# Five RMS norms: squares summed in four column groups of TensorE, three of them applied inside feed-forward units

## The reference

```python
def rmsnorm(x, g):
    xf = x.astype(jnp.float32)
    r = lax.rsqrt(jnp.mean(xf * xf, axis=-1, keepdims=True) + EPS)
    return (xf * r * g.astype(jnp.float32)).astype(x.dtype)

def modulate(h, shift, scale):
    return h * (1.0 + scale[:, None, :]) + shift[:, None, :]
```

## Time and profile before

| | |
|---|---|
| median of 3 runs | 1994.65 us (1994.48 to 1998.07) |
| profiled execution | 1996.98 us |
| its span | 1995.2 us |
| PE busy | 1930.8 us (97%) |
| POOL busy | 1303.9 us (65%) |
| DVE busy | 998.7 us (50%) |
| ACT busy | 805.7 us (40%) |
| mean granted TensorE clock | 0.991 of full speed |

### The profile page before, as it was taken

The page is one execution under the profiler, slowest core; times in us unless marked ns, Lnnn a source line. Parts: engine busy times, 40 slices in busy tenths (PEclk is TensorE's granted clock), DMA queues, the critical chain, the costliest instruction groups (busy, mean ns, idle before and its releaser), DMA issues.

```text
span 1995.2 us, 34548 instructions
## 1 busy us (share of the span) xinstructions
PE 1930.8 (97%) x13934; PEld 1767.5 (89%) x13934; DVE 998.7 (50%) x2150; ACT 805.7 (40%) x872; POOL 1303.9 (65%) x311
## 2 busy tenths in 40 slices
PE   6989899999999999999999898999999999999998
PEld 4879788877676899999999787899999999999998
DVE  6766455675754565445335546433344334654112
ACT  3443344344444543334334424433343334334332
POOL 5726257766667577777775421487758775868784
PEclk8999899999999999999999999999999999999999
DMA  8537167788997656665665311266656665655452
GB/s 348 215 145 274 50 280 305 279 324 324 364 361 271 269 193 252 248 229 219 237 247 201 155 64 64 106 254 239 244 190 252 234 252 190 254 211 211 174 185 85
DMA packets 63958, 448.76 MB, mean 225 GB/s; under 512 B 7680, under 2 KB 8800, under 8 KB 9824
## 3 DMA queue, kind: packets, MB, share of 16 engines
q1 hardware_dynamic: 61888, 441.65, 58.2%
q10 hardware_dynamic: 1952, 5.44, 0.7%
HBM read 446.01 MB, written 1.05 MB: 224 GB/s over the span
## 4 chain that ended last, share of the span: by engine, by line
PE 54%; issue 23%; POOL 18%; DMA 3%; DVE 1%; ACT 1%; POOLq 0%; SPq 0%; ACTq 0%; DVEq 0%
POOL W L670 15%; PE bank L747 11%; PE bank L749 11%; PE bank L748 11%; PE bank L1196 3%; PE bank L1264 3%; PE bank L1197 3%; PE bank L1204 3%; DMA raw<-in_pages 2%; POOL YC L723 1%; PE bank L773 1%; PE bank L782 1%; PE bank L1139 1%; PE bank L793 1%; PE bank L812 1%
## 5 line engine op out<-in xcount | busy, mean ns | idle before, releaser
L670 POOL TENSOR_TENSOR W<-raw,W 128x2048 fp32r<-128x2048 f32 x220 | 1013.7, 4613 | 497.1 <-ACT W L1564 497.0
L747 PE MATMUL bank<-YH,W 128*128 128x256 f32 x1936 | 551.2, 285 | 1.1 <-POOL W L670 0.8
L749 PE MATMUL bank<-YH,W 128*128 128x256 f32 x1936 | 547.6, 283 | 0.0
L748 PE MATMUL bank<-YL,W 128*128 128x256 f32 x1936 | 547.6, 283 | 0.0
L1564 ACT ACTIVATE W<-raw 128x2048 fp32r<-128x2048 f32 x220 | 420.2, 1910 | 302.3 <-PE bank L749 275.6
L747 PEld LDWEIGHTS bank<-YH,W 128*128 128x128 f32 x1936 | 371.0, 192 | 3.9 <-POOL W L670 1.2
L748 PEld LDWEIGHTS bank<-YL,W 128*128 128x128 f32 x1936 | 371.3, 192 | 0.4 <-issue 0.2
L749 PEld LDWEIGHTS bank<-YH,W 128*128 128x128 f32 x1936 | 371.2, 192 | 0.0
L1919 DVE SCALAR_TENSOR_TENSOR bank<-mraw,CA,bank 128x256 f32<-128x256 f32 x696 | 329.0, 488 | 19.8
L2016 DVE TENSOR_TENSOR bank<-bank,SIL 128x256 f32<-128x256 f32 x110 | 47.6, 433 | 541.0 <-ACT SIL L1583 541.0
L747 PE MATMUL bank<-HH,W 128*128 128x256 f32 x880 | 249.7, 284 | 0.5 <-DVE HL L2018 0.4
(11 more groups left out here) (383 smaller groups left out, 3053.2 us busy)
## 6 DMA issues: line engine op xcount, KB each, us to landing
raw<-in_pages SPq DMA_DIRECT2D x284, 1024.0 KB, 4.8
mraw<-in_mpages SPq DMA_DIRECT2D x98, 1024.0 KB, 6.9
R<-in_pages SPq DMA_DIRECT2D x20, 1024.0 KB, 6.9
XR<-in_pages SPq DMA_DIRECT2D x12, 1024.0 KB, 5.5
R<-in_mpages SPq DMA_DIRECT2D x4, 1024.0 KB, 16.5
HT<-in_acts ACTq DMA_DIRECT2D x1, 1024.0 KB, 14.3
CT<-in_mpages SPq DMA_DIRECT2D x1, 1024.0 KB, 19.6
raw<-in_mpages SPq DMA_DIRECT2D x1, 1024.0 KB, 25.4
```

The lines of the kernel that those rows point to most:

```text
L670: nc.gpsimd.tensor_tensor(WL[:, p % SLOTS, :], raw[:, p % SLOTS, :], WH[:, p % SLOTS, :].bitcast(f32), ALU.subtract).then_inc(s_lo, 1)
L747: mm(out, w[0], x[0], start=start, stop=False, skip_group_check=True)
L748: mm(out, w[0], x[1], start=False, stop=False, skip_group_check=True)
L749: return mm(out, w[1], x[0], start=False, stop=stop, skip_group_check=True)
```

## The change

For norms 2 to 6, PE no longer makes eight full 128x128 products with ones. `norm_groups` makes eight products with 32 columns of ones: tile k of the squares goes to the 32 output partitions 32*(k mod 4) and following, so that each group of 32 partitions holds the sum of two tiles. ACT copies the bank to `XR[:, 0, :]` (`norm_groups_copy`), and PE adds the four groups with one full product with ones (`norm_total`). Every value is then 32 times too large, and `norm_root` divides by that.

The parts are placed anew. Norm 2: groups in job 36, copy in job 36, total in job 37; its bank is 7 in place of 5, and PE waits for the last modulation sum of the stage in place of the third scatter. Norm 3: groups after unit 1 of `ctx_ff`, total inside unit 2 between its two gate and up pages. Norm 4: groups after unit 5, total in unit 6, low parts in unit 7. Norm 5: groups after unit 1 of `ff00`, total in unit 2, low parts in unit 3. In such a unit ACT takes the root between the two SiLUs and makes `norm_scaled` (for norm 3 also the squares of norm 4) between its second and third page split; DVE takes the gain between the two hidden halves, and the reciprocal and the eight tiles between the second hidden half and the modulation take and sum. The units that are touched are those whose modulation sum is for one vector. Norm 6: the groups are issued inside `kac0`, after 36 of its 48 matmuls, the total behind `kac0`; ACT takes the root ahead of the copy of `kac0`'s result. The pass `ff00` has two more units written out in place of looped.

```diff
-        tile("ss2", 1, (5,), "act")
+        tile("ss2", 1, (MISC,), "act")
...
+        GROUPED = (2, 3, 4, 5, 6)
+        TOTAL_IN = {("ctx_ff", 2): 3, ("ctx_ff", 6): 4, ("ff00", 2): 5}
+        LOWS_IN = {("ctx_ff", 7): 4, ("ff00", 3): 5}
+        MID_NORM = {"ctx_ff": ((2, "ss3"), (6, "ss4")), "ff00": ((2, "ss5"),), "ff01": (), "ff10": (), "ff11": ()}
...
+            def norm_groups(n):
+                ps = opened(pe, f"ss{n}")
+                pe.wait_ge(s_sq, NCH * (n + 1))
+                for k in range(KD):
+                    rows = slice(GW * (k % NG4), GW * (k % NG4 + 1))
+                    last = mm(ps[rows, 0:S], ONES[:, 0:GW], XR[:, k, :], start=(k < NG4), stop=(k >= KD - NG4),
+                              skip_group_check=True)
+                last.then_inc(s_grp, 1)
+
+            def norm_total(n):
+                pe.wait_ge(s_grpd, GROUPED.index(n) + 1)
+                mm(bank(f"ss{n}")[:, 0:S], ONES[:], XR[:, 0, :], start=True, stop=True, skip_group_check=True)\
+                    .then_inc(s_tile, 1)
...
+                        if behind is not None and b == 1 and k == k_tiles // 2:
+                            behind()
...
+                        if j == 0 and (name, u) in TOTAL_IN:
+                            norm_total(TOTAL_IN[name, u])
...
+                if t == NJOB - 4:
+                    pe.wait_ge(s_macc, MOD_AT["ctx_ff"])
+                    norm_groups(2)
                 if t == NJOB - 3:
-                    pe.wait_ge(s_scd, 4 * (GSLOTS - 2))
-                    norm(2)
+                    norm_total(2)
...
-            ff_pass("ctx_ff", 2, (lambda: mid_norm("ctx_ff", 1, 3), lambda: None, lambda: mid_norm("ctx_ff", 3, 4)))
+            ff_pass("ctx_ff", 2, (nothing, lambda: mid_norm("ctx_ff", 2, 3), nothing, nothing, lambda: mid_norm("ctx_ff", 6, 4)))
...
-            norm(6)
+                   behind=lambda: norm_groups(6)).then_inc(s_tile, 1)
+            norm_total(6)
...
+                copies = GW if n in GROUPED else 1
+                free(f(RT[:, 0:S], ps[:, 0:S], ACT.Sqrt, bias=EPSC[:, 0:1], scale=1.0 / (D * copies)), f"ss{n}")
+
+            def norm_groups_copy(n):
+                act.wait_ge(s_grp, GROUPED.index(n) + 1)
+                f(XR[:, 0, :], bank(f"ss{n}")[:, 0:S], ACT.Copy).then_inc(s_grpd, 1)
...
+                        if (name, u) in TOTAL_IN:
+                            mid = TOTAL_IN[name, u]
+                            if j == 0:
+                                norm_root(mid)
+                            else:
+                                norm_scaled(mid)
+                                if mid == 3:
+                                    norm_squares(4)
...
+                        if j == 0 and (name, u) in TOTAL_IN:
+                            norm_gain(TOTAL_IN[name, u])
+                    if (name, u) in TOTAL_IN:
+                        norm_coef(TOTAL_IN[name, u])
+                        norm_tiles(TOTAL_IN[name, u], range(KD), low=False)
+                    if (name, u) in LOWS_IN:
+                        for q in range(KD):
+                            norm_low(LOWS_IN[name, u], q)
```

More of the change, by code:

```diff
@@ L269, in first_view @@
             return buf.rearrange("p (k n) -> p k n", k=KD)
+        NG4, GW = 4, P // 4
         BY_DVE, BY_PE = (0, 2, 4, 6), (1, 3, 5, 7)
@@ L331, in build @@
         s_sq = sem("norm_squares")
+        s_grp, s_grpd = sem("norm_groups_summed"), sem("norm_groups_copied")
         s_rt, s_ri, s_xr, s_yf, s_y = (sem("norm_root"), sem("norm_coef"), sem("norm_scaled"), sem("norm_result"),
@@ L542, in build @@
                                                             (1, (BOTH, ONE)), (1, (BOTH, BOTH)), (1, (ONE, BOTH)))),
-                ("ff00", FF_UNITS, "y", "acc_00", ((1, (ONE, ONE)), (1, (ONE, ONE)), (FF_UNITS - 2, (ONE, ONE)))),
+                ("ff00", FF_UNITS, "y", "acc_00", ((1, (ONE, ONE)), (1, (ONE, ONE)), (1, (ONE, ONE)), (1, (ONE, ONE)),
+                                                          (FF_UNITS - 4, (ONE, ONE)))),
                 ("ff01", FF_UNITS, "y", "acc_01", ((2, (ONE, ONE)), (FF_UNITS - 2, (ONE, ONE)))),
@@ L814, in tile_page, with linear @@
                 return last
-            def linear(p, ps, x, ready=None, k_tiles=KD, wcol=FU, off=0, inc=True):
+            def linear(p, ps, x, ready=None, k_tiles=KD, wcol=FU, off=0, inc=True, behind=None):
                 w = shaped([a[:, 0:k_tiles * wcol] for a in arrived(p)], "p (k n) -> p k n", k=k_tiles)
@@ L1313, in mid_norm, with nothing @@
                 pe.wait_ge(s_modev, MOD_AT[name] + u - 1)
-                norm(n)
-            ff_pass("ctx_ff", 2, (lambda: mid_norm("ctx_ff", 1, 3), lambda: None, lambda: mid_norm("ctx_ff", 3, 4)))
+                norm_groups(n)
+            def nothing():
+                pass
+            ff_pass("ctx_ff", 2, (nothing, lambda: mid_norm("ctx_ff", 2, 3), nothing, nothing, lambda: mid_norm("ctx_ff", 6, 4)))
             ff_pass("ff00", 4, (lambda: None, lambda: mid_norm("ff00", 2, 5)))
             mod_product(MOD_AT["mixer"] - 1)
-            linear(PA["proj_a"], opened(pe, "kac0"), YC, inc=False, ready=lambda k: y_ready(5, k)).then_inc(s_tile, 1)
-            norm(6)
+            linear(PA["proj_a"], opened(pe, "kac0"), YC, inc=False, ready=lambda k: y_ready(5, k),
+                   behind=lambda: norm_groups(6)).then_inc(s_tile, 1)
+            norm_total(6)
             linear(PA["proj_a"] + 1, opened(pe, "kac1"), YC, inc=False).then_inc(s_tile, 1)
@@ L1545, in norm_root @@
                 ps = filled(act, f"ss{n}")
-                free(f(RT[:, 0:S], ps[:, 0:S], ACT.Sqrt, bias=EPSC[:, 0:1], scale=1.0 / D), f"ss{n}")
+                copies = GW if n in GROUPED else 1
[3 more added lines that the diff above has]
+                f(XR[:, 0, :], bank(f"ss{n}")[:, 0:S], ACT.Copy).then_inc(s_grpd, 1)
             def norm_scaled(n, ks=range(KD)):
@@ L1676, in _, with nothing @@
             after(PA["wout"] + 3)
-            def state_norm():
-                norm_result(3)
-                norm_squares(4)
+            def nothing():
+                pass
             def expert_split(u, part):
@@ L1765, in _ @@
                     norm_squares(2)
+                if t == NJOB - 4:
+                    norm_groups_copy(2)
                 if t == NJOB - 3:
@@ L1777, in _ @@
             norm_squares(3, "acc_moe")
-            ff_pass("ctx_ff", (state_norm, lambda: None, lambda: norm_result(4)))
+            ff_pass("ctx_ff", (nothing, lambda: norm_groups_copy(3), nothing, nothing, lambda: norm_groups_copy(4)))
             norm_squares(5, "acc_ctx")
-            ff_pass("ff00", (lambda: None, lambda: norm_result(5)))
+            ff_pass("ff00", (nothing, lambda: norm_groups_copy(5)))
             norm_squares(6, "acc_00")
@@ L1796, in key_half @@
                 free(f(KA[:, 2 * q:2 * q + 2, c * S:(c + 1) * S], two(filled(act, nm, i)), ACT.Copy), nm, i)
+            norm_groups_copy(6)
+            norm_root(6)
             key_half("kac0", 0, 0, 1)
-            norm_result(6)
+            norm_scaled(6)
             key_half("kac1", 0, 1, 1)
@@ L1950, in norm_low, with norm_gain @@
                                        in1=hi[:, q, :].bitcast(f32), op0=ALU.add, op1=ALU.subtract).then_inc(s_y, 1)
-            def norm_head(n):
+            def norm_gain(n):
                 src, dst, gname, goff, sc, sh, vi = NORMS[n]
@@ L1962, in norm_head @@
                 dve.wait_ge(sem("norm_gain"), n + 1)
+            def norm_head(n):
+                norm_gain(n)
                 if n:
@@ L2422, in _ @@
             residual("acc_moe", (HT, modcol(ADA + 40)))
-            ff_pass("ctx_ff", (lambda: norm(3), lambda: None, lambda: norm(4)))
+            ff_pass("ctx_ff")
             residual("acc_ctx", (CT, half_gate(MOD0 + 16, 1)))
-            ff_pass("ff00", (lambda: None, lambda: norm(5)))
+            ff_pass("ff00")
             residual("acc_00", (HT, half_gate(MOD0 + 16, 0)))
```

1 line of the change is left out of this document (removed).

## The result

The changed kernel took 2005.74 us (median of 5 runs, 2003.83 to 2006.92), the kernel before 1997.16 us beside it (5 runs, 1994.48 to 1998.94). The ratio is 1.0044 with an interval of 1.0033 to 1.0054: slower, by about 9 us or 0.4%, where 1986.5 us (range 1983.8 to 1990.5) had been forecast. The profiled execution took 2004.07 us with a span of 2002.2. Now and then an execution is far slower at a lower granted clock (one of 2376.65 us of the kernel before at 0.749, one of 2694.43 us in experiment 8 at 0.653); the ratios leave such executions out.

What follows compares the result with a forecast made beforehand. PE was taken to bound the feed-forward passes, so its time on norms sets the end. Savings of 0.8 + 5.25 + 0.5 + 1.6 = 8.15 us from 1994.65 gave 1986.5 us, range 1983.8 to 1990.5.

Steps and rivals of the forecast that it cites:

- Does the new place cost anything?: Step timing the moved norm work inside feed-forward units; claimed it stays hidden, with cover 1.1 us in one unit, 3.3 elsewhere.
- The groups: PE's cost per norm: four tiles overlap fully, 0.97 us plus 0.28 for shape change and 0.43 for total, taken as 1.70.
- (a): Rival on PE's groups: four tiles run no faster than two, gain 5.4 us, 1989.3 us; chance 0.18.
- (b): Rival on PE's groups: no overlap with these operands, +3.1 us, 1997.7 us; chance 0.06.
- (c): Rival on PE's groups: each change of tile drains the array, +12.9 us, 2007.5 us; chance 0.04.
- Norms 3 to 5: Feed-forward passes: 1.75 us saved per norm, 5.25 us, plus 0.50 for a wait for the hidden half that goes.
- small waits: Smaller PE waits for the hidden half at norms 4 and 5, left for the range, at most 0.4 us together.
- Norm 2: Passage into `ctx_ff`: PE saves 1.75 us but POOL's end holds it; term 0.8 us, bounds 0 and 1.75.
- Norm 6: Groups inside `kac0`: PE reaches `kac1` earlier and the root, reciprocal, tiles chain moves with it, 1.6 us saved.
- Rival (d): In norm 3 to 5 units: a wait takes the saving back, 1988 to 1992 us, 1990 in the middle; chance 0.10.
- cover: Unit 2 of `ctx_ff`: POOL's low part of the next down page at 22.9, wanted at 24, 1.1 us to spare.
- The sum: Whole kernel: 0.8 + 5.25 + 0.5 + 1.6 = 8.15 us saved, giving 1986.5 us.

Runs made afterwards that it cites:

- experiment 8: Changed kernel with norm 4 and 5 low parts moved from DVE to POOL, plus the edits of experiments 5 and 6: 1987.22 us, 0.995 of the kernel before.
- experiment 4: Changed kernel with the groups made as eight full products on one tile: 2020.40 us, ratio 1.0119 to the kernel before.
- Experiment 1: Changed kernel with norm 4 and 5 low parts taking one operand from a PSUM bank, values wrong: 1988.35 us, 0.9954 of the kernel before.
- experiment 2: Changed kernel with norm 4 and 5 low parts alternating with the tiles in the norm's own unit: 1989.84 us, 0.9968 of the kernel before.
- experiment 3: Changed kernel with POOL's page subtractions from the first feed-forward pass on split in halves: 2007.41 us, ratio 1.0046 to the kernel before.
- experiment 7: Experiment 2 with two groups of 64 in place of four of 32: 1994.22 us, 0.9992 of the kernel before.
- experiment 6: Experiment 2 with a semaphore of its own for ACT's read of `kac0`: 1990.09 us, 0.9974 of the kernel before.
- experiments 5 and 6: The first is experiment 2 with norm 4's squares moved behind ACT's third split: 1988.81 us, 0.9967 of the kernel before; experiment 6 has its own line.

## Why the prediction was wrong

**The step that failed** is "Does the new place cost anything?". It wrote down DVE's tiles at 3.80 us from the earlier trace rows, and the low parts that stand in units 7 and 3 it didn't write down at all. The row was read rightly, but it comes from a stretch in which POOL was idle after the first 0.75 us (and even these show in it, with 0.5 us), and the change moves this work beside POOL, which works 13.9 of 17.8 us in a unit. That an instruction keeps its duration when it is moved was taken for granted; it holds for ACT's squares (2.19 us in both kernels) and PE's full products (3.62 us in experiment 4 as before) and not for DVE with two SBUF operands beside POOL. The eight low parts took 18.05 and 18.45 us in place of about 3.3, DVE's next job was to make `MACC`, and PE waited 6.6 and 6.9 us for it and then worked at the lower clock. Experiment 1 shows the cause by one operand's place, experiment 2 by the time at which the same instructions run. What isn't shown is how the hardware arbitrates; that DVE and POOL take turns by instruction is read from experiment 3 and from the starts in the traces.

**The groups.** Forecast 0.97 + 0.28 us for the groups with the change of shape and 0.43 for the total, 1.68, taken as 1.70; measured 1.19 + 0.43 = 1.62. Of the 0.28 us, the 0.10 was read behind a block of 64 columns (8 instructions at 130.20, ahead of 131.22 in the earlier trace rows) and not of 32; behind the new groups it is 0.11 (694.64 to the next start, 694.87, is 0.23 in place of 0.12), so nothing hangs on it. Rivals (a), (b) and (c) fall: four tiles are faster than two (experiment 7), work runs side by side, and seven changes of tile within the block cost nothing that shows. The figure of the Trainium skill's page "TensorE: Matmul & The Clock Gate", Part 3, 2.38 times for three column tiles, carried on to four, gave an estimate of 1.09 us for the groups. Measured, the 1.07 us hold a tail of 0.38, and the last start and one more distance of 0.216 make about 0.9 us, so here the measurement decides.

**Norms 3 to 5.** Forecast 5.25 + 0.50; by landmarks, the new waits apart, 2.33 + 2.06 + 2.00 = 6.39 us, of which about 0.4 are the small waits that the prediction had left for the range.

**Norm 2.** Forecast 0.8; 2.1 in the changed kernel's profile, but between -0.4 and 2.0 in the profiles of the experiments with four tiles. So one profile can't size this term; that transfers and POOL hold the passage, as the prediction argued from the earlier trace rows, isn't shown.

**Norm 6.** Forecast 1.6, measured 1.27. The reciprocal waits for a count of ACT's reads, and the read of `kac0` (0.59 us) now stands behind the root; experiment 6 gives 1.76 us without that wait.

**Rival (d)** had the right kind, a wait that takes the saving back, but the wrong place and a quarter of the size. Its own mechanism was there too: 1.06 us in unit 3, because the tiles took 6.38 us and overdrew a cover that had been worked out as 1.1.

**The sum** was about right for the mechanism that it described. Without the clash of DVE and POOL the kernel gains 8.8 us (experiment 1, interval 5.8 to 12.6), 7.3 (experiment 2, 4.0 to 8.6) or 8.6 (experiment 8, 7.4 to 12.6, with the edits of experiments 5 and 6 in it), against 8.15 forecast. That it comes so close is in part luck: by the landmarks of experiment 1 the parts are 0.6 (norm 2), 6.4 (norms 3 to 5) and 1.3 us (norm 6) less 1.1 for the wait in unit 3, some 7.1 us together, and the errors of the terms offset each other.

## What to carry to other kernels

When work is moved, read its duration together with what the other engines did at that time: a row measured while POOL was idle isn't the price beside POOL. The hints to look for are an instruction on 8 columns that takes 2.23 us and a group whose first instruction takes 1.03 us and the others 0.47. List for each vector operation that is moved where its operands lie, and ask who else works on SBUF there and what DVE must deliver next. If the clash can't be avoided in time, take one operand out of SBUF (experiment 1 shows what that is worth, not how to get the right values there) or give the work to POOL; cutting POOL's instructions in halves gained nothing.

## What the runs showed of the hardware

DVE and POOL take turns by the instruction where DVE's two tensor operands and POOL's lie in SBUF. With POOL's subtractions back to back, a low part of 0.47 us took 4.84 beside one of 4.6 (which took 4.80 itself), and 2.62 beside a half; the blocks of eight were 18.05 and 18.45 us, and 18.23 with halves. With one operand in a bank the eight took 3.22 us beside the same subtractions.

Four tiles of 32 columns with four-byte operands run fully side by side: 16 instructions in 1.07 us, 1.95 on two tiles of 64 columns, 3.64 on one of 32 and 3.62 with full columns. The two instructions of each product don't hold up those on other tiles.

Waits of PE of 6.6 and 6.9 us cost 2.3 and 3.1 us more behind them, at a granted clock of 0.50 for about 4.5 and 6.2 us.
